# First layer norm of a two-layer flow-matching backbone: tiles transposed, modulated and split one by one beside the second half of the output projection, the last four in two halves

## The reference, cut to what matters

```python
x = layer_norm(DEEPNORM_ALPHA * x + g1 * mix_x, ln1_w[l], ln1_b[l])
x = mlp_sublayer(x, sh2, sc2, g2, w_ff1[l], w_ff2[l], ln2_w[l], ln2_b[l])
# with
def modulate(h, shift, scale): return h * (1.0 + scale) + shift
def mlp_sublayer(h, shift, scale, gate, w1, w2, ln_w, ln_b):
    y = jnp.square(jax.nn.relu(modulate(h, shift, scale) @ w1)) @ w2
    return layer_norm(DEEPNORM_ALPHA * h + gate * y, ln_w, ln_b)
```

## Time and profile before

| | us |
|---|---|
| median of 3 runs | 2935.47 (2933.86 to 2936.0) |
| the profiled execution | 2939.78 |
| its span, first to last instruction | 2937.7 |
| PE busy | 2730.8 (93%) |
| DVE busy | 1947.4 (66%) |
| POOL busy | 1064.3 (36%) |
| ACT busy | 713.4 (24%) |

### The profile page before, as it was taken

The page is one execution under the profiler, slowest core; times in us unless marked ns, Lnnn a source line. Parts: engine busy times, 40 slices in busy tenths (PEclk is TensorE's granted clock), DMA queues, the critical chain, the costliest instruction groups (busy, mean ns, idle before and its releaser), DMA issues.

```text
span 2937.7 us, 36938 instructions
## 1 busy us (share of the span) xinstructions
PE 2730.8 (93%) x13212; PEld 2227.6 (76%) x13212; DVE 1947.4 (66%) x3295; ACT 713.4 (24%) x1454; POOL 1064.3 (36%) x973
## 2 busy tenths in 40 slices
PE   6999998697999999999999699998789999999996
PEld 4777876576888888888887478886577888888885
DVE  4789973756676677677668789863765454454456
ACT  3233324434101111110111323333523111111111
POOL 1344353664111111111112645553763332333325
PEclk9999998798999999999999799998899999999998
DMA  8322322531122222222220212211511111111111
GB/s 238 97 90 68 106 78 78 154 94 43 58 72 72 78 79 71 72 71 72 72 41 25 92 56 62 62 49 47 154 58 61 50 50 43 53 47 49 51 43 65
DMA packets 246651, 214.60 MB, mean 73 GB/s; under 512 B 60384, under 2 KB 203280, under 8 KB 246544
## 3 DMA queue, kind: packets, MB, share of 16 engines
q1 hardware_dynamic: 149488, 120.94, 13.8%
q10 hardware_dynamic: 97056, 92.29, 10.4%
HBM read 190.56 MB, written 22.63 MB: 73 GB/s over the span
## 4 chain that ended last, share of the span: by engine, by line
PE 79%; DVE 9%; DMA 4%; POOL 3%; SPq 2%; issue 1%; ACT 1%; ACTq 0%; POOLq 0%; DVEq 0%
PE bank L571 14%; PE bank L573 14%; PE bank L572 14%; PE bank L1069 9%; PE bank L1070 9%; PE bank L1071 9%; PE bank L651 1%; DMA work<-conv_columns 1%; DVE work L1623 1%; PE bank L977 1%; PE bank L1002 1%; DVE bank L1673 1%; PE bank L1001 1%; PE bank L936 1%; DVE x_hl L1535 1%
## 5 line engine op out<-in xcount | busy, mean ns | idle before, releaser
L1498 POOL TENSOR_TENSOR w_lo<-raw,w_hi 128x1024 fp32r<-128x1024 f32 x120 | 288.2, 2403 | 1118.8 <-ACT w_hi L1332 1118.8
L1069 PE MATMUL bank<-x_hl,w_hi 128*128 128x512 f32 (+1 forms) x1280 | 476.9, 373 | 0.1
L1070 PE MATMUL bank<-x_hl,w_hi 128*128 128x512 f32 (+1 forms) x1280 | 474.1, 370 | 0.0
L1071 PE MATMUL bank<-x_hl,w_lo 128*128 128x512 f32 (+1 forms) x1280 | 473.6, 370 | 0.0
L1768 DVE TENSOR_TENSOR work<-work 128x512 f32<-128x512 f32 (+1 forms) x160 | 157.0, 982 | 474.3 <-ACT work L1320 474.3
L1792 DVE TENSOR_TENSOR work<-work,bank 128x512 f32<-128x512 f32 x576 | 390.1, 686 | 122.3 <-PE bank L573 111.5
L571 PE MATMUL bank<-w_hi,h_hi 128*128 128x512 f32 x1152 | 451.4, 392 | 7.2 <-DVE work L1792 5.3
L572 PE MATMUL bank<-w_lo,h_hi 128*128 128x512 f32 x1152 | 449.6, 390 | 0.0
L573 PE MATMUL bank<-w_hi,h_lo 128*128 128x512 f32 x1152 | 449.5, 390 | 0.0
L1673 DVE SCALAR_TENSOR_TENSOR bank<-work,bank 128x512 f32<-128x512 f32 (+1 forms) x580 | 407.2, 702 | 18.9
L1332 ACT ACTIVATE w_hi<-raw 128x1024 fp32r<-128x1024 f32 x120 | 126.8, 1058 | 783.3 <-PE bank L573 585.1
(11 more groups left out here) (141 smaller groups left out, 4405.6 us busy)
## 6 DMA issues: line engine op xcount, KB each, us to landing
raw<-in_w_ff ACTq DMA_DIRECT2D x128, 512.0 KB
work<-in_w_ada SPq DMA_DIRECT2D x48, 512.0 KB
plain_words<-in_w_ada ACTq DMA_DIRECT2D x64, 256.0 KB
raw<-in_w_in SPq DMA_DIRECT2D x60, 256.0 KB
plain_words<-in_w_ada SPq DMA_DIRECT2D x16, 512.0 KB, 12.6
raw<-in_w_out SPq DMA_DIRECT2D x10, 512.0 KB
gate_rows<-work SPq DMA_DIRECT2D x72, 64.0 KB, 1.6
retention_rows<-work SPq DMA_DIRECT2D x72, 64.0 KB, 1.5
```

Source lines behind the costliest of these rows:

```text
L1069: nc.tensor.matmul(o, slot(mlp_slot(l, f), 0)[:, wc], x_hi[:, k, cols], start=k == 0, stop=False)
L1070: nc.tensor.matmul(o, slot(mlp_slot(l, f), 0)[:, wc], x_lo[:, k, cols], start=False, stop=False)
L1071: mm = nc.tensor.matmul(o, slot(mlp_slot(l, f), 1)[:, wc], x_hi[:, k, cols], start=False, stop=k == KT - 1)
L1498: nc.gpsimd.tensor_tensor(slot(mlp_slot(l, sl), 1), raw[:, un % 2, :], slot(mlp_slot(l, sl), 0).bitcast(F32), ALU.subtract).then_inc(w_rea ...
```

## The change

Tiles of all but the last chunk are no longer taken in steps of a chunk but one by one: three turns behind its projection (from turn 3 on, for the first n - 4 tiles) a tile gets eight transposes into two whole banks, eight modulations and two copies of 512 columns to `x_hi` on ACT, and two subtractions to `x_lo` on DVE. The odd tiles' multiply goes from DVE to POOL, but for the last two tiles, which DVE takes both. The last four tiles keep the steps of a chunk, in two halves of four (`first_block`): in layer 0 the order is hidden products 0, 1, 2, steps 0 to 3, product 3, steps 4 to 7, products 4 and 5; in layer 1 it is product 0, steps 0 to 3, product 1, steps 4 to 7, products 2 and 3. The scaling by alpha goes behind the last hidden product (in layer 0 but for the context tiles').

```diff
-        def by_vector(ln, j):
+        def by_vector(l, ln, j):
-            return j % 2 == 1
+            return j >= len(tiles_of(l)) - 2 if ln == "ln" else j % 2 == 1
+        def tile_banks(j):
+            return (banks[4:6], banks[6:8])[j % 2]
+        def first_block(l):
+            chunks = chunks_of(l)
+            seq = [("hidden", ci, f) for ci in range(len(chunks)) for f in range(2)]
+            seq.insert(-3, ("turn", 0, KT // 2))
+            seq.insert(-2, ("turn", KT // 2, KT))
+            return seq
...
# PE, transpose_step
+                elif which:
+                    pe.wait_ge(S["tile_low"], s0["tile_low"] + len(tiles_of(l)) - 4)
...
# PE, the turns
+                for turn in range(n):
+                    pe.wait_ge(S["z_read"], s0["z_read"] + n + turn - 1)
+                    project(pe, l, IN_UNITS + 4, T[turn], ps_z[turn % 2][:, :], turn == 0, turn == n - 1, S["z_done"])
+                    j = turn - 3
+                    if 0 <= j < n - 4:
+                        pe.wait_ge(S["ln1_done"], s0["ln1_done"] + j + 1)
+                        if j >= 2:
+                            pe.wait_ge(S["tile_low"], s0["tile_low"] + j - 1)
+                        for k in range(KT):
+                            mm = nc.tensor.transpose(tile_banks(j)[k // 4][:, (k % 4) * P:(k % 4 + 1) * P], X[:, T[j], k * P:(k + 1) * P], ident)
+                        mm.then_inc(S["tile_turned"], 1)
...
# PE, hidden
-                            if first and f == 0:
-                                pe.wait_ge(S["split_in"], s0["split_in"] + N_IN0 + KT * ci + k + 1)
+                            if first and f == 0 and ci == len(chunks) - 1:
+                                pe.wait_ge(S["split_in"], s0["split_in"] + N_IN0 + k + 1)
+                            elif first and f == 0 and k == 0:
+                                pe.wait_ge(S["tile_low"], s0["tile_low"] + T.index(t0 + nt - 1) + 1)
...
# ACT, the turns
+                for turn in range(n + 1):
+                    if turn:
                         normalise(l, "ln", turn - 1)
+                    j = turn - 3
+                    if 0 <= j < n - 4:
+                        act.wait_ge(S["tile_turned"], s0["tile_turned"] + j + 1)
+                        for k in range(KT):
+                            turned = tile_banks(j)[k // 4][:, (k % 4) * P:(k % 4 + 1) * P]
+                            last = nc.scalar.activation(turned, turned, ACT.Identity, bias=modc[:, 2, cd, k:k + 1], scale=modc[:, 3, cd, k:k + 1])
+                        last.then_inc(S["tile_mod"], 1)
+                        act.wait_ge(S["tile_mod"], s0["tile_mod"] + j + 1)
+                        for half in range(2):
...
+                        last.then_inc(S["tile_high"], 1)
...
# ACT, first block
+                load(l, IN_UNITS + OUT_UNITS + 2)
+                early = CTX_TILES if l == 0 else 0
+                for kind, a, b in first_block(l):
+                    if kind == "hidden":
+                        hidden(0, 2 * a + b, True)
+                        if early and (a, b) == (0, 1):
+                            scaled(T[:early])
+                    else:
+                        for i in range(a, b):
                             modulate_step(l, 1, i)
+                        if b == KT:
+                            load(l, IN_UNITS + OUT_UNITS + 3)
+                scaled(T[early:])
...
# DVE, the turns, behind the statistics, the shift and the multiply of a turn st
+                    j = st - 4
+                    if 0 <= j < n - 4:
+                        dve.wait_ge(S["tile_high"], s0["tile_high"] + j + 1)
...
+                        last.then_inc(S["tile_low"], 1)
...
# DVE, first block
+                for kind, a, b in first_block(l):
+                    if kind == "hidden":
+                        hidden(0, 2 * a + b, True)
+                    else:
+                        for i in range(a, b):
                             split_step(l, 1, i)
```

More of the change, by code:

```diff
@@ L256, in layer_counts @@
     conv_steps, q_tiles, ret_steps = 4 * runs, PAIRS * NT, PAIRS * n
-    t_in, t_mlp = (1 + runs if l else runs) * KT, runs * KT
+    t_in, t_mlp = (1 + runs if l else runs) * KT, KT
     hidden, shares = 2 * runs * NBLK, 2 * n * NBLK
@@ L594, in in_chunks @@
                 chunks = chunks + [(0, CTX_TILES)]
+            if which:
+                chunks = chunks[-1:]
             return [(t0, n, k) for t0, n in chunks for k in range(KT)]
@@ L621, in last_block, with weighed @@
             return seq
-        def by_vector(ln, j):
-            return j % 2 == 1
[L627 to L639, removed]
+        def by_vector(l, ln, j):
+            return j >= len(tiles_of(l)) - 2 if ln == "ln" else j % 2 == 1
+        def weighed(l, ln, j, vector):
+            return sum(by_vector(l, ln, i) == vector for i in range(j + 1))
+        def tile_banks(j):
[6 more added lines that the diff above has]
+            return seq
         def ada_bank(s):
@@ L1465, in layer_norm_part @@
                             xt = X[:, T[j], :]
-                            if by_vector(ln, j):
-                                pool.wait_ge(S[ln + "_x"], s0[ln + "_x"] + sum(by_vector(ln, i) for i in range(j + 1)))
+                            if by_vector(l, ln, j):
+                                pool.wait_ge(S[ln + "_x"], s0[ln + "_x"] + weighed(l, ln, j, True))
                             else:
@@ L1742, in _ @@
                 nc.vector.tensor_scalar(modc[:, 3, :, :], modc[:, 3, :, :], 1.0, None, ALU.add).then_inc(S["one_added"], 1)
-                for st, steps_now in enumerate(beside_ln1(l)):
+                for st in range(n + 2):
                     if st < n:
@@ L1754, in _ @@
                         ln_weight(l, st - 2, "ln", ln1_rows)
-                    for i in steps_now:
-                        split_step(l, 1, i)
+                    j = st - 4
+                    if 0 <= j < n - 4:
+                        dve.wait_ge(S["tile_high"], s0["tile_high"] + j + 1)
+                        cols = slice(T[j] * P, (T[j] + 1) * P)
+                        for half in range(2):
+                            last = nc.vector.tensor_tensor(x_lo[:, 4 * half:4 * half + 4, cols], tile_banks(j)[half][:, :].rearrange("p (a b) -> p a b", b=P),
+                                                           x_hi[:, 4 * half:4 * half + 4, cols].bitcast(F32), ALU.subtract)
+                        last.then_inc(S["tile_low"], 1)
                 chunks = chunks_of(l)
@@ L1792, in share @@
                             nc.vector.tensor_tensor(X[:, t, hc], X[:, t, hc], gated, ALU.add).then_inc(S["y_read"], 1)
-                for ci in range(len(chunks)):
-                    if ci == len(chunks) - 1:
-                        for i in range(KT * ci, KT * (ci + 1)):
+                for kind, a, b in first_block(l):
+                    if kind == "hidden":
+                        hidden(0, 2 * a + b, True)
+                    else:
+                        for i in range(a, b):
                             split_step(l, 1, i)
-                    hidden(0, 2 * ci, True)
-                    hidden(0, 2 * ci + 1, True)
                 share(0, True)
```

42 lines of the change are left out of this document (13 added, 29 removed).

## The result

| | before | after |
|---|---|---|
| median | 2935.0 (2928.96 to 2940.1, 20 runs) | 2940.22 (2936.34 to 2946.69, 20 runs) |
| the profiled execution | 2939.78 | 2941.92 |
| PE busy | 2730.8 | 2728.8 |
| POOL busy | 1064.3 | 1074.3 |

The ratio is 1.002 with a 95% interval of 1.0014 to 1.0026: the change costs 5.9 us (4.1 to 7.6), for a forecast of 6.4 us above before and a time of 2942.0.

A forecast was written before the change was run, and what follows sets the result against it. PE was taken to bound the kernel, holding 79% of the chain that ended last. Layers +0.8 and clock +5.6 gave +6.4 us: 2946.2 on the profiled execution, 2942 as median; own case 2936.5 to 2948, whole range 2932 to 2949.

The forecast's parts named there:

- The turns: Both layers: PE waits 3.3 us behind turn 3, then 2.35 us at every second tile; layer 1's turn 7 ends 9.8 us later.
- the path of 8.65 us: From a turn's end through DVE and POOL (root, multiply, add) to a finished tile: 8.65 us, 5.4 of them on POOL.
- Tail, layer 1: Behind turn 7: layer norm ends 8.0 us later, the gate's chain follows, step 4 6.2 us later, layer's part ends 6.4 later.
- Tail, layer 0: Behind turn 9, with no gate in the path: the last adds end at 709.3, product 5 at 733.9 for 739.48, 5.6 us gained.
- the sum before the clock: Both layers together, without clock falls: 6.4 us lost in layer 1 less 5.6 gained in layer 0, +0.8 us.
- the taking of turns: In the tails DVE's multiplies and POOL's adds shut each other out and alternate; in layer 1 1.2, 2.4, 1.2, 2.4, 2.4 us.
- The clock: Falls behind PE's waits cost 1.6 us each; both 3.3 us waits certain, three of 2.35 us half: 5.6 us, bounds 0 and 8.0.
- The multiply on POOL: Odd tiles' multiply takes 2.40 us on POOL, 1.22 on DVE; kept on DVE, the sum would be at most 2.4 us lower.
- the clock held: First rival: the full clock holds behind PE's waits in the turns, giving +0.8 us, 2936.3; chance 0.17.
- Tiles ready in time: Rival: the path to a finished tile is under 6.35 us, so no waits or falls in the turns: -12.9 us, 2922.6; chance 0.10.
- a shift caught behind POOL: Rival: DVE's shift stands behind POOL's operation for up to 2.4 us in three turns: +7 on the forecast, 2949; chance 0.08.

The follow-up runs named there:

- filled waits: Changed kernel with useless matmuls of 512 columns put ahead of PE's waits for the finished tile, twelve behind turn 3, eight behind turns 5 and 7: 2934.26 us.
- each layer alone: The change in only one layer, the other as before, against the kernel before: ratio 0.9986 for layer 0 alone, 1.0031 for layer 1 alone.
- unit 2 later: Changed kernel with ACT's split of weight unit 2 behind the modulation of steps 0 to 3, no longer ahead of the first relu: 2931.15 us.
- the odd multiply on DVE: Changed kernel with the odd tiles' multiply back on DVE as before: 2940.27 us, ratio 1.0018 to the kernel before.
- the whole chunk: Changed kernel with the last chunk's eight steps in one piece instead of two halves: 2945.34 us, ratio 1.0029 to the kernel before.
- the tiles asked for later: Changed kernel with each tile's transposes, modulation and subtraction one turn later, four turns behind its projection, POOL's order left as it is: 2916.6 us.
- POOL's order changed: Changed kernel with POOL's multiply and add of tile j ahead of the root of tile j+2 in the first layer norm: 2914.41 us.

## Why the prediction was right, step by step

The end of each step in the changed kernel, moved onto the clock of before (+3.46 us in layer 0, 643.69 - 640.23; +6.36 in layer 1, 2158.05 - 2151.69). To the predicted times 1.6 us are added for each fall that this profile has before that point: three in layer 0, two in layer 1.

| step | predicted | measured |
|---|---|---|
| wait behind turn 3 | 3.3 | 3.23 and 3.25 |
| waits at every second tile | 2.35 | 2.35, 2.33, 2.35 |
| last add of layer 1 ends | 2207.7 + 3.2 = 2210.9 | 2203.63 + 6.36 = 2210.0 |
| gate in use, behind it | 5.4 | 5.48 |
| step 4's transposes, layer 1 | 2224.2 + 3.2 = 2227.4 | 2220.14 + 6.36 = 2226.5 |
| last add of layer 0 ends | 709.3 + 4.8 = 714.1 | 709.34 + 3.46 = 712.8 |
| last relu, layer 1 | 2235.15 + 6.4 + 3.2 = 2244.8 | 2237.66 + 6.36 = 2244.0 |
| last relu, layer 0 | 739.48 - 5.6 + 4.8 = 738.7 | 733.82 + 3.46 = 737.3 |

*The turns* were right to 0.1 us: the path of 8.65 us, asked for after one turn. Two experiments that free PE of the waits by different means got 27.0 and 24.7 us back.

*Tail, layer 1.* The chain ran as described, 0.9 us early from the last add on, and moving the split of unit 2 showed that it sets the end: 9.4 us by the ratios, 6.4 in the profile.

*Tail, layer 0.* It came out 1.4 us better than counted. With layer 1 (0.7 better) the sum before the clock was -1.3 us, not +0.8: (737.3 - 739.5 - 4.8) + (244.0 - 235.15 - 3.2), the second pair without its 2000. Most of these two microseconds stand between the last root and the last add, where DVE's multiplies and POOL's adds take turns (timeline of POOL, layer 0, then the last root of layer 1):

```profile
697.20 0.55 POOL L1494 TENSOR_TENSOR work<-work 128x1 f32<-128x1 f32 x1 [0.93 <-DVE work L1576]
...
700.19 9.15 POOL L1504 TENSOR_TENSOR work<-work 128x1024 f32<-128x1024 f32 x3
...
2191.72 0.55 POOL L1494 TENSOR_TENSOR work<-work 128x1 f32<-128x1 f32 x1 [0.98 <-DVE work L1576]
```

Layer 0 took 709.34 - 697.20 = 12.1 us for it, where 709.3 - 696.0 = 13.3 was counted, and layer 1 2203.63 - 2191.72 = 11.9, for 12.6. So the term that was too large is the taking of turns. In layer 0 the way there was not quite as described: steps 0 to 3 did not wait for the last add, but came right behind product 2, which had waited 3.02 us for the first relus and then took 7.2 us for 5.44, in part at the 1.2 GHz level. From the last add to the last relu it was 24.5 us all the same, for 24.6 counted, and that is in part luck.

*The clock.* The filled waits agree with the price of 1.6 us: 7.9 us for five. The chances of a fall were mis-sized. I called the waits of 3.3 us certain and those of 2.35 us even; this profile fell at all five. Over the six profiled kernels that keep such waits (the changed one, each layer alone, unit 2 later, the odd multiply on DVE, the whole chunk) the next transposes came 7.7 us later or more behind 8 of 10 waits of 3.2 us and behind 14 of 15 waits of 2.3 to 2.4; behind the other three it was 6.4 us, as from 646.14 to 652.54 above. So it is 22 of 25, or 7.0 us for five waits, where I counted 5.6. Against the 6.4 us, 20 of the 22 falls cost 1.5 to 1.7 us, one 1.4 and one, in layer 0 of the kernel with layer 0 alone, 2.8. The two errors, -2.1 us of the tails and +1.4 us of the falls (+2.4 in this profile), nearly cancel, which is why the sum of +6.4 met 5.9 measured and 6.7 in the profile. The mechanism was right, but that the number fits so closely is luck.

*The multiply on POOL* cost no more than the bound of 2.4 us says: 0.6 us, which can't be told from nothing.

*The rivals.* With the clock held, as in the filled kernel, the time is 2.1 us below before (4.7 below to 0.6 above), where the first rival said 0.8 above. That fits the two microseconds of the tails, though the interval alone does not show them. Tiles ready in time were priced at 12.9 us below before; made real, they are worth 18.8 and 21.1 us. 2.1 us of that gap are again the tails. The profiles place the rest. With the tiles asked for later, 0.7 and 0.9 us a layer are left beside the waits and falls; there the last tile's transposes stand behind the last turn and no longer ahead of it, and a turn without them is 6.35 - 5.44 = 0.9 us shorter. With POOL's order changed it is 3.1 and 2.8 us, and there POOL has one multiply and one add less to do behind the last turn. Both reasons fit in size; neither was tested by itself. No wait in the turns came from a shift caught behind POOL.

## What to carry to other kernels

Before work is asked for one stage later than it is made, add up the path through every engine, in their orders, from the event that really releases it: POOL was busy only 5.4 us of 6.35 and still came 2.35 us late, since its work hung on a root of a later turn. First try to change the order of the engine that is late, or the moment of asking; here a few lines of either were worth about 25 us, where a quicker engine for one of the operations gave 0.6 us, not to be told from nothing. And where an instruction waits for a transfer that is not needed yet, see what stands behind it on its engine before moving more work there.

## What the runs showed of the hardware

A wait of PE of 2.3 to 2.4 us was followed by the 1.2 GHz level 14 times in 15, a wait of 3.2 us 8 times in 10, while 2.51 us elsewhere was not the earlier trace rows: in these runs the length of the gap alone does not tell. The fall begins at the transposes or only some matmuls later (the eight transposes took 1.73 us at 645.61 and 1.14 us at 2157.08), and the next tile comes as late in both cases, 8.03 and 8.00 us on. The Trainium skill (TensorE: Matmul & The Clock Gate, What's actually happening) describes a clock that the chip grants in two levels by recent activity, in windows that run on by themselves; that the same wait falls in one execution and not in the next agrees with that.

DVE's operations took longer beside POOL's also on the path that sets layer 1's end. The square and the high part (`CAST`) of the first hidden product took DVE 2.45 us each there, beside POOL's work on the next weights; in layer 0, with POOL idle, the same operations of product 2 took 0.68 and 0.43 us. That is 3.8 us of the chain ahead of step 4, and it is much the same in the kernel before (timeline of DVE in the changed kernel, layer 0, then layer 1):

```profile
713.04 0.68 DVE L1806 TENSOR_TENSOR work<-work 128x512 f32<-128x512 f32 x1
713.76 0.43 DVE L1810 CAST h_hi<-work 128x512 fp32r<-128x512 f32 x1
...
2213.10 2.45 DVE L1806 TENSOR_TENSOR work<-work 128x512 f32<-128x512 f32 x1 [14.03 <-ACT work L1347]
2215.58 2.45 DVE L1810 CAST h_hi<-work 128x512 fp32r<-128x512 f32 x1
```
